# Embedding product moved ahead of the feed-forward part, embedding-gate rows split early, norm transfers issued by ScalarE

## The reference

```python
x = x + rms_norm(mix, ln_mix_post)
h = rms_norm(x, ln_ffn_pre)
f = (silu(h @ w_gate) * (h @ w_up)) @ w_down      # 1024 -> 2816 -> 1024
x = x + rms_norm(f, ln_ffn_post)                  # called x2 below
e = p @ w_ple_proj                                # p: 1024 x 256 per sequence
g = sigmoid(x @ w_ple_gate + b_ple_gate)          # 1024 x 1024
return x + e * g
```

## Time and profile before

| | |
|---|---|
| median of 3 runs | 2580.68 us (2577.84 to 2582.45) |
| the profiled execution | 2580.99 us |
| its span in the trace | 2578.8 us, 2.2 us less |
| busy over the span | PE 93%, DVE 65%, ACT 42%, POOL 35% |
| mean granted TensorE clock | 0.97 of full |

### The profile page before, as it was taken

The page is one execution under the profiler, slowest core; times in us unless marked ns, Lnnn a source line. Parts: engine busy times, 40 slices in busy tenths (PEclk is TensorE's granted clock), DMA queues, the critical chain, the costliest instruction groups (busy, mean ns, idle before and its releaser), DMA issues.

```text
span 2578.8 us, 32820 instructions
## 1 busy us (share of the span) xinstructions
PE 2397.9 (93%) x11528; PEld 1986.6 (77%) x11528; DVE 1681.4 (65%) x1814; ACT 1090.4 (42%) x1607; POOL 903.6 (35%) x549
## 2 busy tenths in 40 slices
PE   7989999698999975999999999899999999969898
PEld 6878878587887764888888888688788888848677
DVE  6678864466888435866766556788888755654732
ACT  4358854433887443333333322444343332233322
POOL 0025521101444122444453356454456535520300
PEclk9999999799999997999999999999999999989999
DMA  4000023510000466544446865755566787464332
GB/s 142 17 26 26 2 106 112 177 33 17 26 9 1 149 170 205 173 136 156 164 139 233 335 247 168 224 192 163 170 219 213 274 330 266 163 249 137 114 83 71
DMA packets 299890, 376.26 MB, mean 146 GB/s; under 512 B 16465, under 2 KB 213969, under 8 KB 299601
## 3 DMA queue, kind: packets, MB, share of 16 engines
q1 hardware_dynamic: 299152, 372.08, 43.0%
q0 software_dynamic: 576, 2.10, 0.2%
HBM read 249.35 MB, written 124.78 MB: 145 GB/s over the span
## 4 chain that ended last, share of the span: by engine, by line
PE 65%; issue 16%; POOL 7%; DVE 4%; DMA 4%; ACT 2%; SPq 1%; POOLq 1%; DVEq 0%; ACTq 0%
PE ps L1180 43%; PE ps L939 19%; PE ps L942 3%; DMA stg<-h_forms 1%; DMA xb<-x_turned 1%; POOL win_s L790 1%; POOL win_s L798 1%; DVE reg L1862 1%; POOL win_s L799 1%; DVE ring L1853 1%; POOL win_s L785 1%; POOL heads L811 1%; SPq L547 1%; POOL wout_a L834 1%; POOL mt_hl L805 1%
## 5 line engine op out<-in xcount | busy, mean ns | idle before, releaser
L1180 PE MATMUL ps<-reg,ring 128*128 128x512 f32 x5544 | 1267.9, 391 | 51.2 <-DVEq L1866 33.1
L1180 PEld LDWEIGHTS ps<-reg,ring 128*128 128x128 f32 x5544 | 1045.1, 189 | 273.5 <-issue 33.3
L1276 ACT ACTIVATE ring<-wraw 128x1024 fp32r<-128x1024 f32 (+2 forms) x152 | 143.6, 946 | 397.8 <-PE ps L1180 372.9
L1853 DVE TENSOR_TENSOR ring<-wraw,ring 128x1024 fp32r<-128x1024 f32 (+2 forms) x152 | 227.4, 1497 | 82.4 <-ACT ring L1276 81.7
L939 PE MATMUL ps<-win,ht 128*128 128x512 f32 (+1 forms) x1152 | 233.4, 361 | 25.9 <-DVE win L1709 25.6
L939 PEld LDWEIGHTS ps<-win,ht 128*128 128x128 f32 x1152 | 190.3, 192 | 57.5 <-DVE win L1709 29.2
L939 PE MATMUL ps<-x2r,gsp 128*128 128x512 f32 x768 | 182.5, 397 | 28.9 <-DVE x2r L2079 20.9
L1276 ACT ACTIVATE ring<-ws 128x1024 fp32r<-128x1024 f32 (+2 forms) x114 | 107.9, 946 | 235.3 <-PE ps L1180 224.1
L1853 DVE TENSOR_TENSOR ring<-ws,ring 128x1024 fp32r<-128x1024 f32 (+2 forms) x114 | 176.1, 1545 | 42.5 <-ACT ring L1276 41.4
L1793 DVE TENSOR_TENSOR pt<-ps,pt 128x512 fp32r<-128x512 f32 x256 | 172.1, 686 | 48.0 <-ACT pt L1276 45.7
L939 PEld LDWEIGHTS ps<-x2r,gsp 128*128 128x128 f32 x768 | 146.7, 192 | 62.6 <-issue 16.8
(11 more groups left out here) (199 smaller groups left out, 3070.0 us busy)
## 6 DMA issues: line engine op xcount, KB each, us to landing
reg<-ff_forms SPq DMA_DIRECT2D x42, 1536.0 KB, 10.0
ff_forms<-fhi SPq DMA_DIRECT2D x88, 512.0 KB, 3.2
wraw<-in_w_gate SPq DMA_DIRECT2D x88, 256.0 KB, 4.2
wraw<-in_w_up SPq DMA_DIRECT2D x88, 256.0 KB, 4.6
ff_forms<-ev SPq DMA_DIRECT2D x44, 512.0 KB, 3.1
wraw<-in_w_down SPq DMA_DIRECT2D x48, 384.0 KB, 5.9
stg<-h_forms SPq DMA_DIRECT2D x28, 512.0 KB, 5.8
reg<-ff_forms SPq DMA_DIRECT2D x14, 1024.0 KB, 5.1
```

The source lines that it names most:

```text
L1180: last = nc.tensor.matmul(ps[:, 2 * chain + m, :], ring[:, st % 3, a, m, k * P:(k + 1) * P], reg[:, k, i, e, :], start=OPENS[i] and k == 0 ...
L1276: copy = lambda out, src, **k: nc.scalar.activation(out, src, ACT.Copy, **k)
L1853: V.tensor_tensor(ring_block(u, st, 1), weight_source(u, i), f(ring_block(u, st, 0)), ALU.subtract).then_inc(S["w_split"], 1)
```

## The change

**Embedding product first.** e = p @ w_ple_proj of both sequences is computed ahead of the first unit. SP first loads w_ple_proj and both p (1 MB each), then the first weights and forms. PE turns the tokens (32 turns), runs the 16 embedding tiles (192 matmuls), ACT copies each from PSUM (`e_tile`) and SP stores it to a new buffer `e_d` (`e_store`); in the tail each tile of e comes back by a load (`e_in`). PE begins the units when all 16 tiles have been copied. The tokens and weights of e lie in memory of `reg` products 4 to 6, so their `fill_hi` waits for the 16 tiles. The copies are woven into ACT's steps -4 to -1 behind `fill_hi`.

**Rows split early.** The x2 rows of sequence 0 are split to high and low halves while the units of sequence 1 run, stored as `x2s_d`, and loaded (1 MB each, `x2_in`) during the seven products of the last unit, into `reg` places that each product has left. The first two gate tiles are loaded and split during the last unit too, and PE interleaves tiles 0 and 1 row by row (`gate_row`). The rows of sequence 0's norm now begin at product 33 of the gate/up units of sequence 1, one each five products.

**Transfers of the norms issued by ACT.** The loads and stores of `norm_in` leave SP's program; ACT issues them between its copies. In the tail the norm of f of sequence 1 works in six slots instead of `fb`: ACT loads four rows (`square_in`), squares them, loads four, squares them, ahead of the first sigmoid; the partition sums are made on PE after tile 3, in two halves that share one buffer (`sumhl`); scaling, adding and splitting of the eight rows go two by two in m = 4..7 (`row_in`, `row_hi`), where also the DVE reciprocal stands (m = 4).

`reg` is laid out product first; the accumulators of the down units lie in its fourth block (`racc`). The numbers of matmuls, of splits and of evictions of the units are unchanged. The core of the diff (left out: semaphore names, buffer declarations, removed functions, and the same accumulator renamed on POOL and DVE):

```diff
+SQ_AT, SPLIT_AT, TOKENS_AT, ROOT_AT, INV_AT, ROW_AT, ROW_STEPS = 7, (23, 25), (25, 27), 28, 29, 33, 5
...
+            def x2_in(k):
+                if k == KT - 1:
+                    sp.wait_ge(S["a_end"], NU - 1)
+                    sp.wait_ge(S["step_done"], NP * (NU - 2))
+                    sp.wait_ge(*at_least("x2s_out", 32 * KT))
+                else:
+                    sp.wait_ge(S["step_done"], NP * (NU - 1) + k + 1)
+                dst = x2_row(0, k).rearrange("p t e n -> p (t e n)").bitcast(F32)
+                sem = on("x2_row") if k == KT - 1 else on(f"op_in{k}")
+                sp.dma_start(dst, x2s_d[:, k].rearrange("p t e n -> p (t e n)")).then_inc(sem, 16)
+            def e_store(m):
+                s, n = divmod(m, KT)
+                sp.wait_ge(*at_least("e_done", m + 1))
+                sp.dma_start(e_d[s, :, n, :], eo[:, m % 2]).then_inc(on(f"e_out{m % 2}"), 16)
...
+            sp.dma_start(pwraw[:], w_proj.rearrange("(k p) n -> p k n", p=P)).then_inc(S["p_in"], 16)
+            for s in range(NSEQ):
+                sp.dma_start(ptok[:, s], p[s * NT:(s + 1) * NT].rearrange("t p n -> p t n")).then_inc(S["p_in"], 16)
             for m in range(2):
                 weights_in(UNITS[0], m)
-            for i in range(2):
+            fill_in(0, 0)
+            weights_in(UNITS[1], 0)
+            for i in range(1, 5):
                 fill_in(0, i)
...
+                    if u.n == NU - 2 and i == 5:
+                        gate_in(0)
+                        gate_in(1)
+                    if u.n == NU - 1:
+                        x2_in(i - 1 if i else KT - 1)
...
+            def embed_tile(m):
+                s, n = divmod(m, KT)
+                bank = 4 * s + 2 * (m % 2)
+                pe.wait_ge(S["pp_split"], s + 1)
+                if m == 0:
+                    pe.wait_ge(*at_least("ps_split", 1))
+                if n >= 2:
+                    pe.wait_ge(*at_least("e_done", m - 1))
...
+            for m in range(2 * KT):
+                embed_tile(m)
+            pe.wait_ge(*at_least("e_done", 2 * KT))
...
+            pe.wait_ge(S["g_split"], 2)
+            for j, k in enumerate(ROWS0):
+                if k == KT - 1:
+                    pe.wait_ge(*at_least("x2_row", 16))
+                else:
+                    pe.wait_ge(*at_least(f"op_in{k}", 16 * (2 * len(DPART) + 1)))
+                for m in range(2):
+                    gate_row(m, k, j == 0, j == KT - 1)
+            turn_y(0)
+            for m in range(2, 2 * KT):
+                pe.wait_ge(S["g_split"], m + 1)
+                pe.wait_ge(S["sig_done"], m - 1)
+                for k in range(KT):
+                    if m == KT:
+                        pe.wait_ge(S["x2_split"], KT + k + 1)
+                    gate_row(m, k, k == 0, k == KT - 1)
+                if m == 3:
+                    for t in range(2):
+                        pe.wait_ge(S["sum_split"], 3 + t)
+                        token_sums(t, sumhl, 4 + t)
+                turn_y(m - 1)
...
+                    if f == 0 and i >= 4 and k == 0:
+                        act.wait_ge(S["proj_done"], 2 * KT)
...
+                n = row_at(u, i, 3)
+                if n is not None:
+                    act.wait_ge(S["x2_sum"], n + 1)
+                    act.wait_ge(*at_least("x2s_out", 32 * n))
+                    copy(stg[:, 2].bitcast(F32R), stg[:, 0]).then_inc(S["x2_hi"], 1)
+                    act.dma_start(x2_d[0, :, n, :], stg[:, 0]).then_inc(S["x2_out"], 16)
...
+            def e_tile(m):
+                s = m // KT
+                act.wait_ge(S["proj_done"], m + 1)
+                act.wait_ge(*at_least(f"e_out{m % 2}", 16 * (m // 2)))
+                copy(eo[:, m % 2], pair(4 * s + 2 * (m % 2))).then_inc(on("e_done"), 1)
...
+                if st == -4:
+                    tokens_hi(1)
+                if -4 <= st < 0:
+                    for m in range(4 * st + 16, 4 * st + 20):
+                        e_tile(m)
+                if inside and u.n == NU - 1 and i in (2, 4):
+                    tile_hi(i // 2 - 1)
...
+            def square_in(n):
+                if n < 6:
+                    for k in range(3):
+                        act.wait_ge(S[f"ev_out{k}"], 16 * EV_OUT[k][NU])
+                    act.wait_ge(S["d_end"], NU)
+                    act.wait_ge(S["f_lo"], 4 * NG * NSEQ)
+                else:
+                    act.wait_ge(S["sq_done0"], n - 5)
+                act.dma_start(chain_slot(n % 6), f_d[1, :, n, :].rearrange("p (t n) -> p t n", t=2))\
+                    .then_inc(on(f"cs_in{n % 6}"), 16)
...
+            def row_in(n):
+                a = 2 * (n % 3)
+                if n >= 3:
+                    act.wait_ge(*at_least(f"cs_out{n % 3}", 16 * (n // 3)))
+                    act.wait_ge(S["x2_split"], KT + n - 2)
+                else:
+                    act.wait_ge(S["sq_done0"], KT)
...
+            def row_hi(n):
+                act.wait_ge(S["x2_sum"], KT + n + 1)
+                act.dma_start(x2_d[1, :, n, :].rearrange("p (t n) -> p t n", t=2), chain_slot(2 * (n % 3)))\
+                    .then_inc(on(f"cs_out{n % 3}"), 16)
+                copy(x2_row(1, n)[:, :, 0], chain_slot(2 * (n % 3))).then_inc(S["x2_hi"], 1)
...
+            for n in range(4):
+                square_in(n)
+            for n in range(4):
+                square(n)
...
+            square_in(6)
+            square_in(7)
+            square_in(4)
+            square_in(5)
+            for n in range(4, KT):
+                square(n)
...
+                if m == 0:
+                    tile_hi(2)
+                elif m + 2 < 2 * KT:
+                    tile_hi(m + 2)
+                if m == 2:
+                    row_in(0)
+                    row_in(1)
+                if m == 3:
+                    act.wait_ge(S["sum_done"], 4)
+                    root(rnorm[:], pair(4), D).then_inc(S["sum_root"], 1)
+                    row_in(2)
+                if 4 <= m < KT:
+                    for k in (2 * m - 7, 2 * m - 6):
+                        if 3 <= k < KT:
+                            row_in(k)
                 if m:
                     y_rows(m - 1)
+                if 4 <= m < KT:
+                    for k in (2 * (m - 4), 2 * (m - 4) + 1):
+                        row_hi(k)
...
+                y_sum(m)
+                if m == 0:
+                    dve.wait_ge(S["sq_done0"], KT)
+                    sum_halves(0, sumhl)
+                if m == 3:
+                    dve.wait_ge(S["sum_done"], 3)
+                    sum_halves(1, sumhl)
...
+                if 4 <= m < KT:
+                    for k in (2 * (m - 4), 2 * (m - 4) + 1):
+                        a = 2 * (k % 3)
+                        t = chain_slot(a)
+                        dve.wait_ge(*at_least(f"cs_in{a}", 16 * row_loads(a, k)))
```

More of the change, by code:

```diff
@@ L1574, in _ @@
                     act.wait_ge(S["step_done"], NP * u.n + 5)
-                    copy(acc[:, acc_at(u, 1)].rearrange("p x n -> p (x n)"), pair(0)).then_inc(S["a_end"], 1)
-                if inside and not u.down and u.seq == 1:
+                    copy(acc_tile(acc_at(u, 1)).rearrange("p x n -> p (x n)"), pair(0)).then_inc(S["a_end"], 1)
+                if inside and norm_at(u, i) >= 0:
                     norm_step(u, i)
@@ new lines, in norm_step @@
+                n, odd = divmod(r - SQ_AT - 2, 2)
+                if 0 <= n < KT and not odd:
+                    use = POST_SQ + n
+                    dve.wait_ge(S["f_sq"], n + 1)
+                    if n == 0:
+                        go(V.tensor_copy(sumsq[:], stg[:, use % 3, :]))
+                    else:
+                        go(V.tensor_tensor(sumsq[:], sumsq[:], stg[:, use % 3, :], ALU.add))
+                    dve.sem_inc(S["stg_free"], 1)
+                if r in SPLIT_AT:
+                    t = SPLIT_AT.index(r)
+                    dve.wait_ge(S["sum_done"], t)
+                    sum_halves(t, sumhl)
@@ new lines, in norm_step, with tile_lo @@
+                n = row_at(u, i, 3)
+                if n is not None:
+                    dve.wait_ge(S["x2_hi"], n + 1)
+                    V.tensor_tensor(stg[:, 1].bitcast(F32R), stg[:, 0], stg[:, 2], ALU.subtract)\
+                        .then_inc(S["x2_split"], 1)
+            def tile_lo(m):
+                dve.wait_ge(S["g_hi"], m + 1)
+                V.tensor_tensor(gsp[:, gate_slot(m), 1], gate_raw(m), f(gsp[:, gate_slot(m), 0]), ALU.subtract)\
+                    .then_inc(S["g_split"], 1)
@@ L2009, in _, with tokens_lo @@
+            def tokens_lo(s):
+                dve.wait_ge(S["pp_hi"], s + 1)
+                for k in range(2):
+                    last = V.tensor_tensor(pturn[:, s, 1, k], pair(4 * s + 2 * k), f(pturn[:, s, 0, k]), ALU.subtract)
+                last.then_inc(S["pp_split"], 1)
+            dve.wait_ge(*at_least("ps_hi", 1))
```

(4 more changed lines are left out.)

558 lines of the change are left out of this document (255 added, 303 removed).

## The result

The changed kernel takes **2600.11 us** (median of 4 runs, 2597.45 to 2602.07) against 2579.92 for the kernel before (4 runs): ratio **1.0077, 95% interval 1.006 to 1.0095**, so slower by some 20 us where a gain of some 8 was forecast. Its profiled execution took 2597.45 us with a span of 2595.6 us. Of the difference, 1.9 us arise ahead of the change: the first transfer of the second part goes out at 975.43 us instead of 973.51.

A forecast was written before the change was run, and what follows sets the result against it. PE's matmuls were taken to bound the units (busy 1261.5 of 1275.3 us), with time lost ahead of them and in the tail. 2580.99 + 40.5 - 0.5 - 48.5 = 2572.5, on the median's scale 2572 us; range 2554 to 2595.

The forecast's parts named there:

- Units, -0.5: Gate/up and down units: norm and row work fits beside PE's matmuls, changing time by -0.5 us (bounds -1.5 and +6).
- Rival B: Units: ACT becomes the gate, waiting for landings, POOL's sum and DVE's subtraction between weight copies; 24 us, 2596; chance 0.13.
- Front, +40.5: Ahead of the units: loading and computing the embedding product there adds 40.5 us (bounds 38 to 52).
- covered with 0.5 to spare: Front, two `eo` buffers: copy, store and landing take 4.9 us against 5.4 for two embedding tiles.
- rival C: Front bound by stores: landings of 5 to 5.5 us add 8 to 12 us, 2580 to 2584; chance 0.12.
- Tail, 250.6: From the units' last matmul to the end: 250.6 us instead of 299.1, a gain of 48.5.
- start: Tail's beginning: PE waits 3.0 us for the last eviction behind a landed store (bounds 1.6 and 8).
- tiles 0 and 1: Tail's first two tiles: 96 matmuls and a cold start take 23.3 us.
- first turn: Tail, before turn_y(0): PE stalls 9.1 us behind ACT's squares and first sigmoid, plus 1.5 cold (bounds 0 and 18).
- token sums: Tail, after tile 3: PE's second sum waits 7.5 us for DVE's `sum_halves(1)`; 9.9 with matmuls and cold start.
- rows of sequence 1: Tail, tiles 4 to 8: row work delays sigmoids and y_sum, losing 29.5 us with cold start (bounds 20 and 37).
- The sum: Whole kernel: 2580.99 + 40.5 front - 0.5 units - 48.5 tail = 2572.5 us.

The follow-up runs named there:

- e3_norow: Changed kernel without the split of the eight x2 rows in the units (high-half copy, low half and their stores left out): 2583.92 us, ratio 1.0007 to the kernel before.
- e9_nostore: Changed kernel without the sixteen stores of the row halves in the units, both halves still computed: 2588.78 us, ratio 1.0023 to the kernel before.
- e5_space: Changed kernel with a row every 7 products instead of 5, each begun at product 1 of a unit: 2586.42 us, ratio 1.0030 to the kernel before.
- f1_all: Changed kernel with e5_space, e8_front and e7_tail joined, and the tail's row sums on DVE: 2533.16 us, ratio 0.9799 to the kernel before.
- e11_sploads: Changed kernel with only each row's two loads in the units, and their waits for the last row's stores, moved to SP: 2603.3 us, ratio 1.009.
- e8_front: Changed kernel with four buffers instead of two for the embedding tiles on their way to memory: 2592.16 us, ratio 1.0043 to the kernel before.
- e4_sums: Changed kernel with the second half of sequence 1's token sums in its own buffer, both halves made right after the squares: 2587.21 us, ratio 1.0022.
- e7_tail: Changed kernel with its tail laid out anew (start, first turn, squares, token sums and rows re-ordered), nothing ahead changed: 2556.92 us, ratio 0.9905.
- e1_layout: Kernel before with only the products' registers laid out product first, so transfers fill 12 KB in a row: 2582.15 us, ratio 1.000.

## Why the prediction was wrong, point by point

- **Units, -0.5: this step failed**, at +17.4. I had added up VectorE's and ScalarE's busy time, "covered as long as the weight copies stay a product (5.4) ahead", and took what is idle for room. The runs show in its place that a row is a round over ACT, DVE and POOL, with the landing of its loads and of its stores in it, that repeats within five products of 5.45 us and delays the weight copies behind it in the engines' order. From the root on, `e3_norow` gives 13.7 us back and `e9_nostore` 9.4; `e5_space` gives 9.1 in its profile, and the same units in `f1_all` 2.2. The low half was listed at "1.22 each, up to 3.4 beside POOL" and then not carried into a place; in the timeline above it is followed by the ring's own half, and without it 3.9 us come back.
- **Rival B** (2596) had the sign and nearly the size. Its holds on ACT exist (6.22 and 6.23 us, two and not one for each row) and are on the chain that ended last, but taken off ACT they gave nothing back (`e11_sploads`): the engine that waits was not the point. Its argument against, the 597 us that ACT waited for PE, doesn't protect: such a sum over 206 waits says nothing of one place in a unit. With a chance of 0.13 I priced it too low.
- **Front, +40.5:** measured 43.8 (45.7 at the same product less 1.9 upstream). The first embedding matmul came at 994.73 (forecast 993), but "covered with 0.5 to spare" failed: the sixteen stores landed in 4.3 us in the median, not in 3.5, ACT idled up to 4.91 us for one (rival C in small), and PE lost 1.63, 0.25, 0.70 and 2.75 us and cold matmuls. `e8_front` confirms the mechanism, with 7 us at the same product.
- **Tail, 250.6:** measured 252.8. By terms: start 6.42 (3.0), tiles 0 and 1 23.8 (23.3), first turn 14.54 (9.1; the fourth row of f landed near 2369.8, 6.5 us later than I had it), token sums 6.40 (7.5), rows of sequence 1 2.90 + 0.54 + 1.42 + 10.88 = 15.7 before cold starts (29.5 with them). So the total is right by luck, by two errors that cancel: 8.9 us too little ahead, and some 7 too much in the middle (tiles 2 to 9 took 126.2 us, 32 more than eight steps of 11.77, where 39.4 were forecast). `e4_sums` and `e7_tail` agree with the mechanisms named for the waits, the second with all of them changed at once.
- **The sum:** 2572.5 + 1.9 upstream + 3.3 front + 17.9 units + 2.2 tail = 2597.8, against 2597.45 measured.
- **Open:** The 2.2 us of the last unit were not taken apart (the first two gate tiles' split and the loads of x2 lie in there). How the 13.7 us of the split divide between the time on the DMA, the holds and DVE's work is argued from the chain and not separated by a run. That the large loads make six products dearer than five is read from two kernels (holds of 14.77 and 14.80 us), not tested by itself. Why the same units take 670.8 us in one profile and 677.7 in another is not known.

## What to carry to other kernels

Work put on idle engines inside a full loop has to be priced as a round, from store to landing to load to next use, against the distance at which it repeats; busy shares tell nothing of it. Here moving such a wait to another queue only handed it on; cutting the stores gave time back, and spacing the rounds did so where the last of them didn't meet larger transfers. A stage that is moved should be looked at where it lands first: here the moved product was worth its price only once the tail that it left behind was laid out anew.

## What the hardware showed unexpectedly

Stores of 0.5 MB, of the kind that lands in 3.5 us in the median before, took 7.1 and 6.8 us among the rows and 21.2 us beside four 1.5 MB loads of the down units, and held ScalarE for 6.2 and 14.8 us. Transfers in rows of 12 KB instead of 4 KB (`e1_layout`) changed the time of the kernel by nothing that can be measured. VectorE's instructions take up to 3.4 us beside GpSimd in the kernel before as well; `e7_tail` shows that this goes on for as long as GpSimd has sums in a row, 10 us for three, while a sum costs VectorE itself 1.2.
